# Recurrent branch of a hybrid decoder layer: norms taken with tokens on partitions and spread back by TensorE

## What is computed

```python
kk = heads(k * p['rwkv_k_k'])
kk = kk / jnp.maximum(jnp.linalg.norm(kk, axis=-1, keepdims=True), 1e-12)
...
xs = tuple(jnp.moveaxis(z, 1, 0) for z in (rh, wh, kh, vh, -kk, kk * ah))
state, ys = lax.scan(step, wkv0.astype(jnp.float32), xs)
y = jnp.moveaxis(ys, 0, 1)
mean = jnp.mean(y, axis=-1, keepdims=True)
var = jnp.mean(jnp.square(y - mean), axis=-1, keepdims=True)
yn = ((y - mean) * lax.rsqrt(var + GN_EPS)).reshape(b, t, B_WIDTH)
yn = yn * p['rwkv_ln_w'].astype(jnp.float32) + p['rwkv_ln_b'].astype(jnp.float32)
...
out = (yn + bonus.reshape(b, t, B_WIDTH)) * g.astype(jnp.float32)
```

## Time and profile before

| | us |
|---|---|
| median of 3 runs (3174.07 to 3187.11) | 3178.32 |
| the profiled execution | 3194.11 |
| its span | 3192.3 |
| PE busy, of the span | 2627.6 |
| DVE busy | 1375.7 |
| ACT busy | 521.6 |
| mean granted clock of PE | 0.891 |

### The profile page before, as it was taken

One profiled execution on the slowest core, in us unless ns is written; L12 is line 12 of the kernel. 1 busy time (PEld: TensorE's weight loads), 2 busy tenths in 40 slices (PEclk: granted clock), 3 DMA queues, 4 the chain that ended last, 5 costly groups with the idle time before them and its releaser, 6 DMA issues. The chain is left out here.

```text
span 3192.3 us, 52672 instructions
## 1 busy us (share of the span) xinstructions
PE 2627.6 (82%) x21805; PEld 1855.1 (58%) x21805; DVE 1375.7 (43%) x2828; ACT 521.6 (16%) x1067; POOL 75.9 (2%) x119
## 2 busy tenths in 40 slices
PE   4645899993787787877577777899599999999995
PEld 2334566662554555556354454556388888888884
DVE  2042299995236172362445445130343343333433
ACT  3020000002032130221243343000110000100102
POOL 0000000001000000000101000000000000000000
PEclk7765999996889888887798898999799999999998
DMA  3112322214123031220465563440111111111101
GB/s 112 57 31 58 132 68 68 82 48 129 47 59 97 24 97 50 71 78 20 130 222 171 187 221 126 142 140 20 40 40 40 40 40 40 40 40 45 48 14 56
DMA packets 281972, 253.14 MB, mean 79 GB/s; under 512 B 53403, under 2 KB 232189, under 8 KB 281622
## 3 DMA queue, kind: packets, MB, share of 16 engines
q1 hardware_dynamic: 203438, 176.63, 18.3%
q10 hardware_dynamic: 78312, 73.34, 7.5%
HBM read 201.32 MB, written 48.59 MB: 78 GB/s over the span
## 5 line engine op out<-in xcount | busy, mean ns | idle before, releaser
L322 PE MATMUL ps_pr<-hT,w_pr 128*128 128x384 f32 (+1 forms) x1248 | 390.1, 476 | 21.5 <-DMA w_pr<-in_w_in 21.5
L322 PEld LDWEIGHTS ps_pr<-hT,w_pr 128*128 128x128 f32 x1248 | 239.5, 192 | 172.1 <-issue 17.1
L1014 PE MATMUL rwkv_banks<-h_chunk,w_gate 128*128 128x384 f32 (+1 forms) x768 | 304.9, 544 | 19.0 <-ACT gate_rows L1355 8.5
L1014 PEld LDWEIGHTS rwkv_banks<-h_chunk,w_gate 128*128 128x128 f32 x768 | 158.5, 218 | 114.8 <-issue 52.5
L2559 DVE TENSOR_TENSOR x<-x,ps_ml 128x272 f32<-128x272 f32 x224 | 97.6, 436 | 268.6 <-PE ps_ml L2524 268.6
L2524 PE MATMUL ps_ml<-h_mlp,w_ml 128*128 128x272 f32 x768 | 183.7, 396 | 27.4 <-DMA w_ml<-in_w_mlp_in 27.4
L2524 PEld LDWEIGHTS ps_ml<-h_mlp,w_ml 128*128 128x128 f32 x768 | 147.4, 192 | 58.7 <-DMA w_ml<-in_w_mlp_in 27.9
L2524 PE MATMUL ps_ml<-hidden,w_ml 128*128 128x272 f32 x768 | 181.2, 392 | 0.0
L768 DVE TENSOR_SCALAR_CACHE_REDUCE above<-scores,mid 128x384 f32<-128x384 f32 (+1 forms) x180 | 170.2, 946 | 6.4
L2550 ACT COPY hidden<-ps_ml 128x272 f32<-128x272 f32 x128 | 49.3, 385 | 698.7 <-PE ps_ml L2524 698.7
L2524 PEld LDWEIGHTS ps_ml<-hidden,w_ml 128*128 128x128 f32 x768 | 145.9, 190 | 30.1
(11 more groups left out here) (421 smaller groups left out, 3951.9 us busy)
## 6 DMA issues: line engine op xcount, KB each, us to landing
k_pages<-in_cache_k SPq DMA_DIRECT2D x128, 256.0 KB, 3.1
v_pages<-in_cache_v SPq DMA_DIRECT2D x128, 256.0 KB, 3.9
w_gate<-in_w_in ACTq DMA_DIRECT2D x48, 512.0 KB, 4.3
w_ml<-in_w_mlp_in SPq DMA_DIRECT2D x32, 512.0 KB, 5.3
w_ml<-in_w_mlp_out SPq DMA_DIRECT2D x32, 512.0 KB, 4.6
proj_T<-stage_pr ACTq DMA_DIRECT2D x26, 548.0 KB, 3.9
w_pr<-in_w_in SPq DMA_DIRECT2D x25, 512.0 KB, 3.9
gates<-gates_T ACTq DMA_DIRECT2D x16, 544.0 KB, 3.9
```

Source lines behind the costliest of these rows:

```text
L322: ins = self.nc.tensor.matmul(self.ps[0:width, slot % 2, c, 0:m], w[:, k, 0:width], rhs[:, k, t0:t0 + m], start=(k == 0), stop=(k == slice ...
L1014: ins = MM(B[:, GB, 0:w], gw[:, n % 2, k, :], hc[:, k, 0:w], start=(k == 0), stop=(k == KO - 1))
```

## The change

Squares are summed with the squares as the stationary operand, 128 tokens at a time (`sums_by_token`): the moving operand is two columns of `halves`, one per head, so that the sums come out with tokens on the partitions, 18 columns for nine tiles of tokens. ScalarE takes the root of these columns (one instruction for the eight full tiles, one for the sample's 64 tokens), VectorE their reciprocal, and TensorE spreads them over the channels again (`spread`): for each tile and head a matmul whose stationary operand is the one column, repeated 64 times, and whose moving operand is the identity. VectorE multiplies by the result out of PSUM. In the key norm two of the scaled operands are made ahead of the scaling of `kk`; in `normalise` the weight goes with the scaling and the bias with the bonus.

```diff
+    inv = sb("norm_of_tokens", [128, 2, 2 * (NI + 1)])
...
+            ch.done(nc.gpsimd.memset(inv[:, :, :], 1.0))
...
+            TILES = [(t, 128 if t < NI else TS) for t in range(NI + 1)]
+
+            def sums_by_token(t, w):
+                return MM(B[0:w, LO, 2 * t:2 * t + 2], nrm[:, t * 128:t * 128 + w], p.halves[:, 0:128:64], start=True,
+                          stop=True)
+
+            def spread(n, sem):
+                for t, w in TILES:
+                    for h in range(2):
+                        ins = MM(B[HS[h], LO + t // 3, (t % 3) * 128:(t % 3) * 128 + w],
+                                 inv[0:w, n, 2 * t + h:2 * t + h + 1].to_broadcast([w, 64]), p.ident[0:w, 0:w],
+                                 start=True, stop=True)
+                    if t % 3 == 2:
+                        ins.then_inc(S[sem], 1)
+
             def prelude(i):
                 if i:
-                    pe.wait_ge(S["gn_root"], i * 3)
+                    pe.wait_ge(S["gn_scaled"], i * 3)
...
                 pe.wait_ge(S["act_sq"], i + 1)
-                for c_, (t0, w) in enumerate(CH):
-                    MM(B[:, LO + c_, 0:w], p.halves[:, :], nrm[:, t0:t0 + w], start=True, stop=True)\
-                        .then_inc(S["pe_ss"], 1)
+                for t, w in TILES:
+                    ins = sums_by_token(t, w)
+                ins.then_inc(S["pe_ss"], 1)
                 gate(16)
+                pe.wait_ge(S["kk_inv"], i + 1)
+                spread(0, "kk_back")
...
                 pe.wait_ge(S["s_ok"], i * 2 + 2)
-                for c_, (t0, w) in enumerate(CH):
-                    pe.wait_ge(S["gn_sq"], i * 3 + c_ + 1)
-                    MM(B[:, LO + c_, 0:w], p.halves[:, :], nrm[:, t0:t0 + w], start=True, stop=True)\
-                        .then_inc(S["gn_var"], 1)
+                for t, w in TILES:
+                    if t % 3 == 0:
+                        pe.wait_ge(S["gn_sq"], i * 3 + t // 3 + 1)
+                    ins = sums_by_token(t, w)
+                ins.then_inc(S["gn_var"], 1)
                 for c_, (t0, w) in enumerate(CH):
                     MM(B[:, HI + c_, 0:w], g2[:, i * 128:i * 128 + 128], gd[:, t0:t0 + w], start=True, stop=True)\
                         .then_inc(S["pe_g"], 1)
+                pe.wait_ge(S["gn_inv"], i + 1)
+                spread(1, "gn_back")
                 gate(4)
...
-                for c_, (t0, w) in enumerate(CH):
-                    act.wait_ge(S["pe_ss"], i * 3 + (3 if c_ == 0 else c_ + 1))
-                    nc.scalar.activation(nrm[:, t0:t0 + w], B[:, LO + c_, 0:w], ACT.Sqrt).then_inc(S["act_nrm"], 1)
+                act.wait_ge(S["pe_ss"], i + 1)
+                for w, a, b in ((128, 0, 2 * NI), (TS, 2 * NI, 2 * NI + 2)):
+                    nc.scalar.activation(inv[0:w, 0, a:b], B[0:w, LO, a:b], ACT.Sqrt).then_inc(S["act_nrm"], 1)
...
-                dve.wait_ge(S["act_nrm"], i * 3 + 3)
-                ch.done(V.tensor_scalar(nrm[:, :], nrm[:, :], 1e-12, None, ALU.max))
-                ch.done(V.reciprocal(nrm[:, :], nrm[:, :]))
-                ch.done(V.tensor_tensor(kk[:, :], kk[:, :], nrm[:, :], ALU.mult))
+                dve.wait_ge(S["act_nrm"], i * 2 + 2)
+                ch.done(V.tensor_scalar(inv[:, 0, :], inv[:, 0, :], 1e-12, None, ALU.max))
+                V.reciprocal(inv[:, 0, :], inv[:, 0, :]).then_inc(S["kk_inv"], 1)
                 dve.wait_ge(S["act_exp"], i * 4 + 4)
+                ch.mark(V.tensor_tensor(ar[:, 1, :], r, e1[:, :], ALU.mult))
+                ch.mark(V.tensor_tensor(kt[:, :], kn[:, :], e3[:, :], ALU.mult))
+                for c_, (t0, w) in enumerate(CH):
+                    dve.wait_ge(S["kk_back"], i * 3 + c_ + 1)
+                    V.tensor_tensor(kk[:, t0:t0 + w], kk[:, t0:t0 + w], B[:, LO + c_, 0:w], ALU.mult)\
+                        .then_inc(S["kk_scaled"], 1)
...
-                ch.done(V.reciprocal(nrm[:, :], nrm[:, :]))
-                ch.done(V.tensor_tensor(y[:, :], y[:, :], nrm[:, :], ALU.mult))
-                ch.done(V.tensor_scalar(y[:, :], y[:, :], vs[:, 5:6], vs[:, 6:7], ALU.mult, ALU.add))
+                V.reciprocal(inv[:, 1, :], inv[:, 1, :]).then_inc(S["gn_inv"], 1)
+                for c_, (t0, w) in enumerate(CH):
+                    dve.wait_ge(S["gn_back"], i * 3 + c_ + 1)
+                    V.scalar_tensor_tensor(out=y[:, t0:t0 + w], in0=y[:, t0:t0 + w], scalar=vs[:, 5:6],
+                                           in1=B[:, LO + c_, 0:w], op0=ALU.mult, op1=ALU.mult).then_inc(S["gn_scaled"], 1)
...
-                ch.done(V.tensor_tensor(y[:, :], y[:, :], bon[:, :], ALU.add))
+                ch.done(V.scalar_tensor_tensor(out=y[:, :], in0=y[:, :], scalar=vs[:, 6:7], in1=bon[:, :], op0=ALU.add,
+                                               op1=ALU.add))
```

More of the change, by code:

```diff
@@ L903, in rwkv @@
         "pool_dif": 8, "pe_za": 6, "act_sa": 6, "pe_g": 3, "c_ready": 1, "act_exp": 4, "kk_raw": 1,
-        "act_sq": 1, "pe_ss": 3, "act_nrm": 3, "rk_made": 1, "pe_bon": 3, "bon_done": 3, "tilde": 1, "round_made": 1,
-        "gn_mean": 3, "gn_sub": 3, "gn_sq": 3, "gn_var": 3, "gn_root": 3,
+        "act_sq": 1, "pe_ss": 1, "act_nrm": 2, "kk_inv": 1, "kk_back": 3, "kk_scaled": 3, "rk_made": 1, "pe_bon": 3, "bon_done": 3, "tilde": 1, "round_made": 1,
+        "gn_mean": 3, "gn_sub": 3, "gn_sq": 3, "gn_var": 1, "gn_root": 2, "gn_inv": 1, "gn_back": 3, "gn_scaled": 3,
         "a_made": 4, "a_kept": 8, "p_made": 2 * LV + 2, "p_kept": 2 * LV, "x_made": 2 * LV + 2, "x_kept": 2 * LV,
@@ L1281, in _ @@
                 pe.wait_ge(S["bon_done"], i * 3 + 3)
-                pe.wait_ge(S["act_nrm"], i * 3 + 3)
                 for g in range(4):
@@ L1437, in _ @@
             load_gate(1)
-            act.wait_ge(S["pool"], 2)
+            act.wait_ge(S["pool"], 3)
             for i in range(HP):
@@ L1480, in _ @@
                     nc.scalar.activation(nrm[:, t0:t0 + w], y[:, t0:t0 + w], ACT.Square).then_inc(S["gn_sq"], 1)
-                for c_, (t0, w) in enumerate(CH):
-                    act.wait_ge(S["gn_var"], i * 3 + (3 if c_ == 0 else c_ + 1))
-                    nc.scalar.activation(nrm[:, t0:t0 + w], B[:, LO + c_, 0:w], ACT.Sqrt, bias=eps_gn[:, 0:1],
+                act.wait_ge(S["gn_var"], i + 1)
+                for w, a, b in ((128, 0, 2 * NI), (TS, 2 * NI, 2 * NI + 2)):
+                    nc.scalar.activation(inv[0:w, 1, a:b], B[0:w, LO, a:b], ACT.Sqrt, bias=eps_gn[0:w, 0:1],
                                          scale=1.0 / 64).then_inc(S["gn_root"], 1)
@@ L1533, in prelude @@
                                        op1=ALU.mult).then_inc(S["rk_made"], 1)
-                dve.wait_ge(S["act_nrm"], i * 3 + 3)
-                ch.done(V.tensor_scalar(nrm[:, :], nrm[:, :], 1e-12, None, ALU.max))
-                ch.done(V.reciprocal(nrm[:, :], nrm[:, :]))
-                ch.done(V.tensor_tensor(kk[:, :], kk[:, :], nrm[:, :], ALU.mult))
+                dve.wait_ge(S["act_nrm"], i * 2 + 2)
+                ch.done(V.tensor_scalar(inv[:, 0, :], inv[:, 0, :], 1e-12, None, ALU.max))
+                V.reciprocal(inv[:, 0, :], inv[:, 0, :]).then_inc(S["kk_inv"], 1)
                 dve.wait_ge(S["act_exp"], i * 4 + 4)
+                ch.mark(V.tensor_tensor(ar[:, 1, :], r, e1[:, :], ALU.mult))
[4 more added lines that the diff above has]
+                        .then_inc(S["kk_scaled"], 1)
+                dve.wait_ge(S["kk_scaled"], i * 3 + 3)
                 ch.mark(V.scalar_tensor_tensor(out=ar[:, 0, :], in0=kk[:, :], scalar=-1.0, in1=e2[:, :], op0=ALU.mult,
                                                op1=ALU.mult))
-                ch.mark(V.tensor_tensor(ar[:, 1, :], r, e1[:, :], ALU.mult))
-                ch.mark(V.tensor_tensor(kt[:, :], kn[:, :], e3[:, :], ALU.mult))
                 ch.wait()
@@ L1688, in normalise @@
                 dve.wait_ge(S["gn_sub"], i * 3 + 3)
-                dve.wait_ge(S["gn_root"], i * 3 + 3)
-                ch.done(V.reciprocal(nrm[:, :], nrm[:, :]))
-                ch.done(V.tensor_tensor(y[:, :], y[:, :], nrm[:, :], ALU.mult))
-                ch.done(V.tensor_scalar(y[:, :], y[:, :], vs[:, 5:6], vs[:, 6:7], ALU.mult, ALU.add))
+                dve.wait_ge(S["gn_root"], i * 2 + 2)
+                V.reciprocal(inv[:, 1, :], inv[:, 1, :]).then_inc(S["gn_inv"], 1)
[3 more added lines that the diff above has]
+                                           in1=B[:, LO + c_, 0:w], op0=ALU.mult, op1=ALU.mult).then_inc(S["gn_scaled"], 1)
+                dve.wait_ge(S["gn_scaled"], i * 3 + 3)
                 dve.wait_ge(S["bon_done"], i * 3 + 3)
-                ch.done(V.tensor_tensor(y[:, :], y[:, :], bon[:, :], ALU.add))
+                ch.done(V.scalar_tensor_tensor(out=y[:, :], in0=y[:, :], scalar=vs[:, 6:7], in1=bon[:, :], op0=ALU.add,
+                                               op1=ALU.add))
                 for c_, (t0, w) in enumerate(CH):
```

## The result

| | before | the change |
|---|---|---|
| median us (20 runs each) | 3185.84 (3174.07 to 3196.78) | 3193.10 (3186.88 to 3200.79) |
| profiled execution, span us | 3192.3 | 3188.5 |
| ratio, 95% interval | | 1.0026 (1.0015 to 1.0037) |

(The ratio is not the quotient of the two medians, which is 1.0023.) The prediction was 3177 in a range up to 3193, so the time lies just outside, on the slow side. Nearly half of the distance is the reference: its 20 runs have a median of 3185.8, the three that were shown had 3178.3. The rest is a cost of 7 us where -1 was predicted.

The account below looks back on a forecast made before the run. It took TensorE as the bound (busy 2627.6 of 3192.3 us), VectorE mattering only where waited for. Terms +6.0 - 2.2 - 10.0 + 7.5 - 2.4 = -1.1 us, from the median 3178.3, gave 3177; range 3161 to 3193.

Parts of the forecast that it names:

- key norm, work and clock: Four key norms: +6.0 us of added TensorE work, and +7.5 from three more clock falls behind the narrow sums.
- boundaries, work less waits, and clock: Variance to next round, three times: waits of 6.7 us go, less added TensorE work, -2.2; low clock behind them goes, -10.0.
- stage end: Last round: VectorE's chain no longer ends it; TensorE's gates, 1.5 us later, end it at 1548.9: -2.4 us.
- Sums on TensorE: Each of eight places: three wide matmuls, 1.82 us, become 18 narrow passes at 1.1 us, upper end 2.0.
- a clock term: Key norm: the clock falls behind the sums in all four rounds, three more than now, 2.5 us each: +7.5, least certain.
- the spread: Each of eight places: 36 TensorE passes spreading values back over channels, 2.2 us, from 1.9 to 3.65.
- rival C: The spread's two halves do not overlap: 1.45 us more at eight places, +11.6, total 3189; chance 0.08.
- no wait at the rate product: Boundaries: no TensorE wait for VectorE before the second decay/rate product; the 8 gate steps behind it take 5.4 us at 1.00.
- no new wait on TensorE: Key norm and variance: TensorE does not wait for the new small reciprocals, nor the products for VectorE's tildes.
- A: Key norm: the clock stays as it is, without the +7.5 us; total 3170; chance 0.27.
- B: The clock changes at neither key norm nor boundaries: sum +1.4 us, total 3180; chance 0.08.
- D: Small matmuls lower the clock wherever they stand, also inside the busy variance: seven more falls, +24.5 us, total 3204; chance 0.07.

Follow-up runs that it names:

- second series: The kernel before and the change, both unaltered, run again for second profiles: ratios 0.9996 and 1.0006 to the kernel before.
- the square first: ScalarE's key square moved ahead of keeping gate block 12i, in the kernel before and in the change: 0.9956 and 0.9966 of the kernel before.
- four steps ahead: The change with 4 gate steps moved from behind the key norm's sums to ahead of them: 3168.05 us, 0.9950 of the kernel before.

## Why the prediction was wrong, and what of it was right

By the segments, each profile of the change against one of the kernel before:

| | predicted | first pair | second pair |
|---|---|---|---|
| key norm, work and clock | +6.0 + 7.5 = +13.5 | +14.0 | +13.6 |
| boundaries, work less waits, and clock | -2.2 - 10.0 = -12.2 | -8.8 | -5.4 |
| stage end | -2.4 | -1.6 | -0.6 |
| stage start | 0 | -0.1 | -0.6 |
| sum | -1.1 | +3.5 | +7.0 |

By the ratios it is +8.3 and, in the second series, about +2.

Taken apart: from the key sums to the products the two kernels with the square first differ by 144.2 - 133.8 = +10.4, and no clock falls behind their sums. But this segment holds one more low clock, behind the wait for `h_chunk` in round 1, where 8 gate steps take 5.4 us at full clock. The kernel before and the change, both with the square first:

```profile
996.56 7.24 PE L1014 MATMUL rwkv_banks<-h_chunk,w_gate 128*128 128x384 f32 x16 [6.80 <-DMA h_chunk<-h_T]
997.68 8.41 PE L1016 MATMUL rwkv_banks<-h_chunk,w_gate 128*128 128x384 f32 x16 [6.74 <-DMA h_chunk<-h_T]
```

Less these 1.2 us, the key norm's work is +9.2. The clock behind its sums is +5.3 in the first pair (7.0 against 1.7) and +3.5 in the second (8.6 against 5.1), that behind `h_chunk` -0.5 and +1.0 (7.59 against 8.07, 7.89 against 6.86), and these add up to the +14.0 and +13.6. At a boundary, from the sums to the decay product, TensorE needs 8.94 us (947.12 to 956.06 in the change) where it needed 6.33 (948.69 to 955.02): three times 2.61, less 6.7 of waits, is +1.1; the clock gives -9.7 against the profile I read and -6.5 against the second.

The step that failed is the first: "Sums on TensorE", 1.1 us. They take 2.0, the stated upper end. I had taken L576 as the nearest row, because its moving part is as small. But L576's weights are 64 rows high, its matmuls alternate between rows 0 to 63 and 64 to 127, and in the trace its passes start in pairs, 0.007 us apart, a pair every 0.21: two of them pass side by side. The sums are full height. What I called "even smaller here", the moving part, does not matter (2 or 32 columns, the same 2 us). The right row was the one I put down as the bound, L1105 of full height at 0.11. Nor does the halving rescue L576: the same passes at the lower level take 0.206, so 0.113 at that level is not our pass but half of one. The term stands at eight places, 0.9 us each: 7 us, which takes the sum from -1.1 to about +6. (Some 0.3 us more a place goes to neighbours: the output gate takes 2.03 us from start to start for 1.83, the gate steps 2.77 for 2.68.) In the key norm this was hidden by a clock term too large by 2 to 4 us: I priced each fall at 2.5, and seven of the eight seen in the change cost 1.7. That the key norm's total came out right, +13.5 for +14.0 and +13.6, is luck. At the boundaries the step shows.

Right were: that the key norm's reciprocal is worth nothing (0.9996 without it); the spread (2.16 for 2.2, so its halves overlap and rival C is out); no wait at the rate product, and 5.4 us behind it at 1.00; no new wait on TensorE; and that the clock falls in all four key norms, so rivals A and B are out. D is out for the change, since the output gate behind the sums runs clean, but with less room than I gave it: 4 us of such passes would have done it. The drain at a switch of tiling mode that the Trainium skill warns of (TensorEngine Tiling, Key Properties) is within the spread's 2.16 us and the 0.09 that the gate steps behind it lost.

I had counted the clock's falls in one profile, which had an unlucky boundary (9.7 us, 6.5 in the next profile) and a lucky key norm (one fall in four, where 11 in 20 is usual). The median of three runs, 7.5 us below that of twenty, was the other half of the miss: the range should have been as wide as the reference itself was uncertain.

One sentence of mine was true and still missed the point: TensorE's wait of 2.4 us for the squares stays. It stayed, and the change made the low clock behind it worse. Its cause, the place of one instruction in ScalarE's order, is worth 14 us, more than the whole change costs.

Still open: why 1.0026 and 1.0006, beyond chance; and what decides whether a given wait is followed by the lower clock (1.81 us ahead of the rate product was in most rounds, but not in round 2 of the kernel with the square first).

## What to carry to other kernels

A matmul that swaps its operands to have few moving columns pays for the weights instead: in this kernel 0.11 us at full clock for every pass with 128 columns of full height in f32. Look for a row with the same height, not the same width. Reciprocals that nobody waits for cost nothing. Before rewriting arithmetic, ask of each wait on the busy engine what the releasing engine did ahead of it: here a wait of constant length came from its order. And price the clock from several executions: a fall that one profile shows may be missing in the next.

## What the runs showed of the hardware

Two microseconds of 2-column matmuls at full clock left it alone inside busy work (2.03 us for the output gate behind them in every variance of the change), four microseconds did not (3.15 to 3.92). Two of them behind a wait of 2.4 us were followed by the lower level each time (8 of 8 key norms in two profiles of the change), the wide matmuls behind the same wait in 11 of 20, and the narrow ones without the wait in none of 8 (the change with the square first, and with four steps ahead).

The large scatter lies where the change does nothing, and it goes with the clock. From the first products of the last round to its mean sums, in the kernel before and the same again:

```profile
1401.35:1531.34 129.99, 102.39 (x2829) 76.56 (x2829) 36.80 (x84) 20.54 (x54) 0.00 (x0) 0.78 0.10 25
1393.37:1517.98 124.61, 97.86 (x2829) 73.35 (x2829) 36.78 (x84) 20.55 (x54) 0.00 (x0) 0.82 0.09 25
```

The number of instructions and the busy time of VectorE and ScalarE are the same, the granted clock is 0.78 and 0.82; over the four rounds TensorE is busy for 401.8 us of 514.1, and for 390.0 of 503.0.

Another limit stands in the same place. In the triangular levels TensorE gets through 128 matmuls and 128 weight loads in almost the same time, busy for 2.7 to 3.4 us of it; three stretches in a row, cut at its idle times, from the kernel before:

```profile
1021.38:1025.38 4.00, 2.85 (x128) 2.32 (x127) 3.49 (x6) 0.00 (x0) 0.00 (x0) 1.00 0.41 131
1025.38:1029.32 3.94, 3.35 (x128) 2.38 (x128) 1.18 (x3) 0.65 (x2) 0.00 (x0) 1.00 0.02 4
1029.32:1033.32 4.00, 2.65 (x128) 1.95 (x128) 1.09 (x3) 0.65 (x2) 0.00 (x0) 1.00 0.01 4
```

The idle time between them has no releaser in the trace. But it comes by the count of instructions: of the 34 such idle times over 0.3 us in the stage, 30 stand a multiple of 256 TensorE instructions (give or take 4) behind the one before. And instructions are fetched in packets of 16 KB, of which one starts some 1.7 us after the start of each of the three stretches. Part 3 of the page counts them (packets, MB, share of the DMA engines):

```profile
q8 instruction: 166, 2.72, 0.3%
```

These idle times add up to 52.0 us, and to 52.6 in the kernel before, again, so the 11 us between those two are not theirs. The Trainium skill (Runtime: NRT & Kernel Launch, Instruction fetch mechanics) says that fetching instructions is hidden behind their issue; these rows speak for the contrary, but no run here tested it.
